# A mixture-of-experts tail: the first expert's rows before most slabs, the last small expert joined on chip

## The chip, the cores and the metric

One core of one Trainium2 chip runs the whole kernel in one launch. The metric is the device time of that launch in microseconds, lower is better. TensorE, VectorE, ScalarE, GpSimd and SyncE each run their own stream of instructions and meet at semaphores; GpSimd and SyncE mostly issue DMAs.

## The reference

Two layers of a hybrid decoder on 512 prompt tokens and 8 sample tokens of width 1024. The mixers (windowed attention, gated linear attention) and the dense feed-forward of layer 0 are as before and untouched. The second layer ends in a mixture of 8 experts of which each token uses 2:

```python
def _moe(h, rw, rb, wg, wu, wd):
    logits = (h @ rw + rb).astype(jnp.float32)
    top_v, top_i = lax.top_k(logits, TOP_K)
    probs = jax.nn.softmax(top_v, axis=-1)
    gates = jnp.sum(jax.nn.one_hot(top_i, N_EXPERTS, dtype=jnp.float32) * probs[..., None], axis=1).astype(h.dtype)
    out = jnp.zeros_like(h)
    for e in range(N_EXPERTS):
        out = out + gates[:, e:e + 1] * _swiglu(h, wg[e], wu[e], wd[e])
    return out
...
    x = x + g2 * f.reshape(b, s, d)
```

## The kernel before

`x` stays in SBUF, features on partitions: [128, 8, 520], 512 prompt columns and 8 sample columns. All matrix products with weights are done three times with operands split into a high and a low part: each slab of weights (128 x 1024, 512 KB) is loaded, ScalarE copies its high part, VectorE subtracts to get the low part, TensorE multiplies.

The experts (`experts(l)` in each engine's block) work on rows, not on all tokens. The experts are ranked by how many tokens chose them; the four larger ones get 256 rows, the four smaller ones 128. A DRAM tensor `slots` holds 384 rows for each pair of a large and a small expert. A program value `n_sweeps` says how often all experts are gone through, once for these inputs. The steps:

1. TensorE turns the normalised tokens to rows, VectorE writes them to `hT` (five blocks, L1730), GpSimd writes these to `h_rows` in DRAM (L594) and gathers the first expert's 256 rows from there into `xs` (two indirect DMAs, L598). Then it scatters all rows, twice each, to `slots` (ten indirect DMAs, L606).
2. SyncE loads an expert's 33 slabs into a ring of 11 buffers (`raw` for three, `more` for eight, L491). A slab goes into its buffer when the slab 11 before it has been split (`slab_low`). `first_slabs` loads the first three slabs of an expert as soon as its number is known; it stands before the loop and once more at the end of each sweep, where it loads three slabs that nobody multiplies.
3. TensorE turns `xs` (`to_features`, L762), ScalarE and VectorE split it into `XE`. In `expert(i, half)` TensorE does 22 slabs of gate and up products (L802), turns the hidden rows (L782), and 11 slabs of down products (L820) into the PSUM banks 4 to 7. In between (`next_features`) it turns the rows of the expert that comes next, also in the last one. The splits run ahead of TensorE by at most six slabs, and by at least three (`AHEAD`).
4. The result `Yo_large` or `Yo_small` is evacuated (L1374, L1849), GpSimd writes it back to `slots` (L619), after which it fetches the `xs` of the next large expert (L617).
5. After the last small expert GpSimd gathers for each block of 128 tokens (`TAIL`: the samples first) the two rows of each token from `slots` into `Yg` (L625). ScalarE scales one by its gate (L1384), VectorE adds the other (L1858), TensorE turns the sum (L836), VectorE multiplies by the modulation and adds to `x` (L1873), GpSimd writes the block to the output `yT` (L631).

Each engine goes through its own list in the order of the code, and a wait holds back all that stands behind it on that engine.

Of the kernel before, what the change touches and what calls it, by code (L numbers as in the profile page):

```python
# [14 lines left out]
F32 = mybir.dt.float32  # L15
# [87 lines left out]
def build(nc, xT, cT, wst, cst, sml, wa2, kcT, vc, st, yT, kp, vp, sp_, ks, vs, ss):  # L103
    ctx = ExitStack()
    with ctx:
# [25 lines left out]
        def fixed(name, shape, dt=F32):  # L131
# [66 lines left out]
        sweeps = at("sweeps", [P, 1], I32, H0 + 31680)  # L198
# [26 lines left out]
        Yg = [[at(f"Yg{n}{q}", [P, D], F32, (B0 + 8192 * n if n < NB else Z0) + 4096 * q)  # L225
               for q in range(CHOICES)] for n in range(NB + 1)]
        ysm = at("ysm", [P, KT, NS], F32, Z0 + 8192)
# [150 lines left out]
        TAIL = (NB,) + tuple(range(NB))  # L378
# [79 lines left out]
        def _(sp):  # L458
# [42 lines left out]
            n_sweeps = sp.value_load(sweeps[0:1, 0:1], min_val=1, max_val=3)  # L501
            with sp.Fori(0, n_sweeps) as c:
# [5 lines left out]
                first_slabs(c + 1)  # L508


        @block.gpsimd
        def _(pool):
# [97 lines left out]
            n_sweeps = pool.value_load(sweeps[0:1, 0:1], min_val=1, max_val=3)  # L610
            with pool.Fori(0, n_sweeps * RANKS) as i:
                for half in range(2):
                    pool.wait_ge(sem("xt_done"), i * 6 + (4 + 2 * half))
                    if half == 0:
                        pool.dma_start(xs[:, 0:1, :], slot_rows(i * PAIR_ROWS + CAPS[0], 1)).then_inc(sem("xs_in"), 16)
                    else:
                        pool.dma_start(xs[:], slot_rows(i * PAIR_ROWS + PAIR_ROWS, 2)).then_inc(sem("xs_in"), 16)  # L617
                    pool.wait_ge(sem("Yo_made"), i * 3 + (3 + half))
                    pool.dma_start(slot_rows(i * PAIR_ROWS if half == 0 else (i + 1) * PAIR_ROWS - CAPS[1], 2 - half), Yo[half][:]).then_inc(sem("Yo_out"), 16)  # L619
                    pool.wait_ge(sem("Yo_out"), i * 32 + (16 + 16 * half))  # L620

            for n in TAIL:
                rows = block_rows(n)
                for q in range(CHOICES):
# [3 lines left out]
            for n in range(NB):  # L628
                pool.wait_ge(sem("x_final"), n + 2)
                cols = slice(n * P, n * P + P if n + 1 < NB else N)  # L630
                pool.dma_start(yT[:, :, cols], x[:, :, cols]).then_inc(sem("y_out"), 16)  # L631
# [9 lines left out]
        def _(pe):  # L641
# [95 lines left out]
            def experts(l):  # L737
# [31 lines left out]
                def expert(i, half):  # L769
# [23 lines left out]
                    for c in range(CHUNKS):  # L793
                        cols = chunk_cols(c)
                        pe.wait_ge(sem("hel_made"), i * (2 * CHUNKS) + (c0 + c + 1))
                        for k in range(4 * c, chunk_end(c) + 1):
# [12 lines left out]
                            if half == 1 and k in (10, 12, 14, 16):  # L809
                                next_features((k - 10) // 2)  # L810
# [1582 lines left out]
```

## Time and profile before

| | us |
|---|---|
| median of 3 timed runs | 1932.15 (1929.97 to 1937.15) |
| profiled execution | 1930.32 |
| its span | 1928.8 |
| TensorE busy in it | 1823.4 (95%) |
| VectorE, ScalarE, GpSimd busy | 996.9, 810.8, 115.5 |
| mean granted TensorE clock | 0.969 |

The span is from the first to the last instruction; the execution is 1.5 us longer. The share of TensorE is a mean over a long product part and two short parts around the experts in which it waits. A granted clock of 1.00 is 2.4 GHz, 0.50 is 1.2 GHz. Times of an instruction overlap with those of its neighbour where an engine is pipelined, so the distance of starts is what a series costs.

### The profile page before, as it was taken

Reading aid. Unit: us, or ns where it says so; the run is one execution under the profiler, and the core shown is the slowest. Engines: PE = TensorE matmul, PEld = TensorE weight load, DVE = VectorE, ACT = ScalarE, POOL = GpSimd, SP = SyncE. Lnnn points to the kernel's source line nnn. Section 1 sums busy time; section 2 is a strip of 40 time slices with the busy share of each in tenths; the row PEclk is TensorE's granted clock in tenths of the full one; section 3 lists DMA queues with packets and bytes.
Section 4 is the critical chain, followed back from the end, with each engine's and each line's share of the span. In section 5 each row is a group of like instructions: output and inputs, shape, how many; then the busy total and the mean of one; then the engine's idle time right before and its main releaser. Section 6 shows DMA issues by size and latency. Waiting matters only on the chain.

```text
span 1928.8 us, 33321 instructions
## 1 busy us (share of the span) xinstructions
PE 1823.4 (95%) x13468; PEld 1638.8 (85%) x13468; DVE 996.9 (52%) x1380; ACT 810.8 (42%) x1192; POOL 115.5 (6%) x170
## 2 busy tenths in 40 slices
PE   6999999999999999999999999959999999999993
PEld 4888999998998999989889999948878878878872
DVE  4367552745222323335675527455495495495483
ACT  3346524323221122224465243225375385385471
POOL 1000010001101100000000100020000000000002
PEclk8999999999999999999999999969999999999996
DMA  9832235247676742224222342166596596596574
GB/s 376 346 113 91 97 135 199 89 153 252 223 254 205 252 164 88 86 80 154 69 88 100 135 177 100 45 270 235 174 371 239 174 360 244 179 348 250 185 283 143
DMA packets 96905, 362.94 MB, mean 188 GB/s; under 512 B 12212, under 2 KB 12244, under 8 KB 94992
## 3 DMA queue, kind: packets, MB, share of 16 engines
q1 hardware_dynamic: 65376, 238.94, 34.7%
q0 software_dynamic: 31408, 122.27, 17.6%
q8 instruction: 90, 1.47, 0.3%
q14 instruction: 31, 0.25, 0.0%
HBM read 310.80 MB, written 50.36 MB: 187 GB/s over the span
## 4 chain that ended last, share of the span: by engine, by line
PE 81%; DMA 7%; DVE 4%; issue 3%; ACT 3%; SPq 1%; POOL 0%; POOLq 0%; ACTq 0%; DVEq 0%
PE ps L650 46%; PE ps L802 16%; PE ps L820 9%; DMA xs<-slots 2%; PE ps L842 2%; DMA g<-gates 2%; DMA slots<-Yo_large 1%; DMA first_ada<-weights 1%; PE ps L762 1%; SPq L464 1%; PE ps L782 1%; PE ps L1080 1%; ACT scb L1491 1%; PE ps L958 1%; PE ps L970 0%
## 5 line engine op out<-in xcount | busy, mean ns | idle before, releaser
L650 PE MATMUL ps<-Hh,wh 128*128 128x260 f32 x2080 | 604.4, 291 | 9.4 <-ACT qrt L1520 5.3
L650 PE MATMUL ps<-Hl,wh 128*128 128x260 f32 x2080 | 592.9, 285 | 0.0
L650 PE MATMUL ps<-Hh,wl 128*128 128x260 f32 x2080 | 592.0, 285 | 0.0
L650 PEld LDWEIGHTS ps<-Hh,wh 128*128 128x128 f32 x2080 | 397.1, 191 | 29.5 <-issue 28.6
L650 PEld LDWEIGHTS ps<-Hh,wl 128*128 128x128 f32 x2080 | 397.3, 191 | 0.0
L650 PEld LDWEIGHTS ps<-Hl,wh 128*128 128x128 f32 x2080 | 396.9, 191 | 0.2
L1673 DVE TENSOR_TENSOR wl<-raw,wh 128x1024 fp32r<-128x1024 f32 x168 | 205.5, 1223 | 337.8 <-ACT wh L1305 337.4
L1305 ACT ACTIVATE wh<-raw 128x1024 fp32r<-128x1024 f32 x168 | 177.2, 1055 | 215.6 <-PE ps L650 212.6
L802 PE MATMUL ps<-further,XE 128*128 128x512 f32 (+1 forms) x840 | 189.2, 378 | 0.0
L802 PE MATMUL ps<-wh,XE 128*128 128x512 f32 (+1 forms) x592 | 181.8, 379 | 1.9 <-issue 1.9
L802 PEld LDWEIGHTS ps<-further,XE 128*128 128x128 f32 x840 | 146.6, 188 | 29.1
L1807 DVE TENSOR_TENSOR wl<-more,wh 128x1024 fp32r<-128x1024 f32 x96 | 115.8, 1223 | 42.4 <-ACT wh L1332 42.1
L1807 DVE TENSOR_TENSOR further<-more,further 128x1024 fp32r<-128x1024 f32 x96 | 115.9, 1224 | 36.6 <-ACT further L1332 36.5
L802 PEld LDWEIGHTS ps<-wh,XE 128*128 128x128 f32 x592 | 109.4, 190 | 21.6 <-issue 2.3
L1332 ACT ACTIVATE wh<-more 128x1024 fp32r<-128x1024 f32 x96 | 99.8, 1056 | 41.5 <-PE ps L802 22.3
L802 PE MATMUL ps<-wl,XE 128*128 128x512 f32 (+1 forms) x296 | 110.9, 375 | 0.0
L650 PE MATMUL ps<-hidh,wh 128*128 128x260 f32 x352 | 101.3, 288 | 4.8 <-issue 3.2
L1332 ACT ACTIVATE further<-more 128x1024 fp32r<-128x1024 f32 x96 | 99.7, 1055 | 14.1 <-PE ps L820 8.4
L650 PE MATMUL ps<-hidl,wh 128*128 128x260 f32 x352 | 99.4, 282 | 0.0
L650 PE MATMUL ps<-hidh,wl 128*128 128x260 f32 x352 | 99.3, 282 | 0.0
L820 PE MATMUL ps<-further,heh 128*128 128x512 f32 x256 | 81.2, 398 | 0.0
L650 PEld LDWEIGHTS ps<-hidh,wh 128*128 128x128 f32 x352 | 66.3, 188 | 10.4 <-DVE hidl L2256 5.5
(407 smaller groups left out, 2627.4 us busy)
## 6 DMA issues: line engine op xcount, KB each, us to landing
raw<-weights SPq DMA_DIRECT2D x243, 512.0 KB, 3.5
more<-weights SPq DMA_DIRECT2D x192, 512.0 KB, 5.2
ada<-weights POOLq DMA_DIRECT2D x16, 1536.0 KB, 8.1
slots<-nothing POOLq DMA_DIRECT2D x28, 704.0 KB, 12.8
first_ada<-weights POOLq DMA_DIRECT2D x8, 2048.0 KB, 12.5
gates<-stage POOLq DMA_DIRECT2D x32, 260.0 KB, 2.8
first_ada<-weights SPq DMA_DIRECT2D x16, 512.0 KB, 16.0
g<-gates POOLq DMA_DIRECT2D x2, 3120.0 KB, 12.4
```

Of the source, the lines that this page charges most:

```text
L464: sp.dma_start(first_slab(m), wst[m, :, :]).then_inc(ada_full[m], 16)
L650: mm = pe.matmul(out, w, v[:, cols], start=first and q == 0, stop=last and q == 2)
L762: mm = pe.transpose(ps[:, 4 + r, k * P:k * P + P], xs[:, r // 2, (4 * (r % 2) + k) * P:(4 * (r % 2) + k) * P + P], ident)
L782: mm = pe.transpose(ps[:, 2 * (c % 2), (b * tiles + t) * P:(b * tiles + t) * P + P], hmm[:, c % 2, t, b * P:b * P + P], ident)
L802: mm = pe.matmul(ps[:, 2 * (c % 2) + t, 0:cols], X[:, v, kk, t * P:t * P + P], w[:, b * cols:b * cols + cols], start=kk == 0 and r == 0, s ...
L820: mm = pe.matmul(ps[:, 4 + 2 * t + q, :], v[:, k, t * P:t * P + P], w[:, q * 512:q * 512 + 512], start=k == 0 and r == 0, stop=k == FE - 1 ...
L842: mm = pe.matmul(ps[STRIP * j:STRIP * j + STRIP, bank, 0:SCOLS], c_pad[:, m % CHUNK, :], w[:, j * SCOLS:j * SCOLS + SCOLS], start=m % CHUN ...
L958: mm = pe.transpose(ps[:, 6, h * P:h * P + P], scb[t % 4][:, h, c * P:c * P + P], ident)
L1305: act.activation(wh[:, sl, :], raw[:, sl, :], ACT.Copy).then_inc(hi_made[sl], 1)
L1332: act.activation(split_pair(k % SPLITS)[0], ring(k % EXP_SLABS % RING), ACT.Copy).then_inc(sem("slab_high"), 1)
L1673: dve.tensor_tensor(wl[:, sl, :], raw[:, sl, :], wh[:, sl, :].bitcast(F32), ALU.subtract).then_inc(split_made[sl], 1)
L1807: dve.tensor_tensor(w_l, ring(k % EXP_SLABS % RING), w_h.bitcast(F32), ALU.subtract).then_inc(sem("slab_low"), 1)
```

## The change

On SyncE one wait is added between the first three slabs and the rest, and the output is written by SyncE in four parts. On the other engines the last pair of experts is written out apart from the loop (`final=True`):

- During the last large expert VectorE works out, from row numbers and gates, for each token whether one of its two rows lies in the last small expert's 128 rows (`last_rows`): `w_others` are the gates with those rows set to 0, `last_of` is a token by row matrix holding the gate at the row's place. TensorE turns it and ScalarE copies it to `last_to` (128 rows x 520 tokens).
- The gathers from `slots` follow the write of `Yo_large`, before the last small expert's rows have been multiplied. The samples' gather waits until TensorE has finished the gate and up products, since it lands in `XE[1]`.
- The last small expert turns no next rows, and the last three splits are left out. ScalarE and VectorE scale and mix `Yg` with `w_others` after their last split.
- After the last product TensorE turns `Yg` into banks of 512 tokens each, and multiplies `Yo_small`, straight from SBUF, by `last_to`; VectorE adds both to `x`, 512 columns at a time.

```diff
             first_slabs(0)
             sp.wait_ge(sem("order_made"), 1)
             n_sweeps = sp.value_load(sweeps[0:1, 0:1], min_val=1, max_val=3)
+            sp.wait_ge(sem("xs_in"), 32)
             with sp.Fori(0, n_sweeps) as c:
...
                 first_slabs(c + 1)
+            sp.wait_ge(*dve_tail("samples_final"))
+            for k in range(0, KT, 2):
+                sp.wait_ge(*dve_tail(f"x_final{k + 1}"))
+                sp.dma_start(yT[:, k:k + 2, :], x[:, k:k + 2, :]).then_inc(sem("y_out"), 16)
+            sp.wait_ge(sem("y_out"), 16 * (KT // 2))
...
+            with pool.Fori(last, last + 1) as i:
+                small_rows(i, True)
+            for n in range(NB + 1):
                 rows = block_rows(n)
+                if n == 0:
+                    pool.wait_ge(*pe_tail("last_turned"))
+                if n == NB:
+                    pool.wait_ge(*pe_tail("gates_done"))
...
                     pe.wait_ge(sem("XE_made"), i * 6 + (4 + 2 * half))
+                    if final and half == 0:
+                        pe.matmul(ps[:, 6, 0:P], ones, MSK, start=True, stop=True).then_inc(sem("pe_tail"), 1)
...
-                            if half == 1 and k in (10, 12, 14, 16):
+                            if half == 1 and k in (10, 12, 14, 16) and not final:
                                 next_features((k - 10) // 2)
-
-                    pe.wait_ge(sem("XE_made"), i * 6 + (6 + 4 * half))
+                            if final and half == 0 and k == 8:
+                                pe.wait_ge(*dve_tail("last_of_made"))
+                                for n in range(NB):
+                                    pe.transpose(ps[:, 7, n * P:n * P + P], last_of[:, n, :], ident)
+                                pe.transpose(ps[:, 6, 0:NS], last_of[0:NS, NB, :], ident[0:NS, 0:NS]).then_inc(sem("pe_tail"), 1)
...
+                for n in range(NB):
+                    pe.wait_ge(sem("f_made"), n + 1)
+                    for k in range(5):
+                        main_turned(n, k)
+                pe.wait_ge(sem("f_made"), NB + 1)
+                for k in range(KT):
+                    mm = pe.transpose(ps[:, 7, k * NS:k * NS + NS], Yg[NB][0][0:NS, k * P:k * P + P], ident[0:NS, 0:NS])
+                mm.then_inc(sem("pe_tail"), 1)
+                pe.wait_ge(sem("Yo_made"), last * 3 + 4)
...
+                for k in range(5, KT):
+                    if k > 5:
+                        pe.wait_ge(*dve_tail(f"x_main{k - 6}"))
+                    for n in range(NB):
+                        main_turned(n, k)
+                for k in range(KT):
+                    if k in (0, 4):
+                        pe.wait_ge(*dve_tail("samples_final" if k else "samples_main"))
+                    else:
+                        pe.wait_ge(*dve_tail(f"x_main{k + 1 if k < 4 else k}"))
+                    pe.matmul(ps[:, LAST_BANK[k], :], Yo[1][:, 0, k * P:k * P + P], last_to[:, 0:T], start=True, stop=True
+                              ).then_inc(sem("pe_tail"), 1)
...
                     for k in range(EXP_SLABS):
-                        slab_high(i, s0 + k + AHEAD)
+                        if not (final and half and k + AHEAD >= EXP_SLABS):
+                            slab_high(i, s0 + k + AHEAD)
...
-                dve.tensor_scalar(sweeps[:], posv[8][:, 0, 0:1], 1.0, None, ALU.add).then_inc(sem("order_made"), 1)
+                link(dve.tensor_scalar(sweeps[:, 1:2], posv[8][:, 0, 0:1], float(RANKS), float(RANKS - 1), ALU.mult, ALU.add))
+                dve.tensor_scalar(sweeps[:, 0:1], posv[8][:, 0, 0:1], 1.0, None, ALU.add).then_inc(sem("order_made"), 1)
...
+                    for n in range(NB + 1):
+                        rows = block_rows(n)
+                        link(dve.tensor_scalar(last_of[0:rows, n, :], ps[0:rows, 6, 0:P], at_last[0:rows, n:n + 1], None, ALU.is_equal))
+                        mm = dve.tensor_scalar(last_of[0:rows, n, :], last_of[0:rows, n, :], w_last[0:rows, n:n + 1], None, ALU.mult)
+                    mm.then_inc(sem("dve_tail"), 1)
...
+                        if final and half == 0 and k == 2:
+                            last_rows()
...
+                def added(bank, k):
+                    return dve.scalar_tensor_tensor(out=x[:, k, 0:T], in0=ps[:, bank, :], scalar=mod[:, l, 5 * KT + k, 0:1],
+                                                    in1=x[:, k, 0:T], op0=ALU.mult, op1=ALU.add)
```

SyncE at the entry, before the change (`ISA` rows hold a wait or set up a DMA; the line numbers are those of each kernel):

```order
L491 DMA raw<-weights 128x1024
L501 TENSOR_LOAD sweeps [waits order_made]
L501 ISA x2
L502 UNCONDITIONAL_BRANCH
L504 TENSOR_LOAD eids
L504 ISA x2
L506 ISA
L491 ISA [waits slab_low]
```

and with it:

```order
L513 DMA raw<-weights 128x1024
L523 TENSOR_LOAD sweeps [waits order_made]
L523 ISA x2
L525 UNCONDITIONAL_BRANCH [waits xs_in]
L527 TENSOR_LOAD eids
L527 ISA x2
L529 ISA
L513 ISA [waits slab_low]
L513 DMA more<-weights 128x1024
```

The first slab for `more` now stands behind a wait for `xs_in`, the gathered rows.

GpSimd at the exit, before the change:

```order
L619 ISA [waits Yo_made]
L619 DMA slots<-Yo_small 128x1024
L620 REGISTER_ALU
L611 ISA [waits Yo_out]
L611 COMPARE_AND_BRANCH
L625 DMA Yg_180<-slots,rowi 8x1024
L625 DMA Yg_181<-slots,rowi 8x1024
L625 DMA Yg_172<-slots,rowi 128x1024
...
L631 DMA yT<-x 1024x1x128 [waits x_final] x3
L631 DMA yT<-x 1024x1x136 [waits x_final]
```

and with it:

```order
L642 DMA xs<-slots 128x1024
L644 REGISTER_ALU
L645 ISA [waits xt_done]
L646 ISA [waits Yo_made]
L646 DMA slots<-Yo_large 128x2x1024
L647 ISA
L656 ISA [waits Yo_out]
L656 COMPARE_AND_BRANCH
L665 DMA Yg_172<-slots,rowi 128x1024 [waits pe_tail]
L665 DMA Yg_173<-slots,rowi 128x1024
...
L665 DMA Yg_180<-slots,rowi 8x1024 [waits pe_tail]
```

The gathers follow the write of `Yo_large`, not of `Yo_small`; the fetch of two tiles of `xs` and the writes of `yT` are gone from GpSimd.

TensorE after the last product, before the change (L836 turns `Yg`):

```order
L820 MATMUL ps<-further_166,hel 128x512
L836 MATMUL ps<-cs,Yg_180 128x8 [waits f_made]
L836 MATMUL ps<-cs,Yg_180 128x8 x7
L836 MATMUL ps<-cs,Yg_172 128x128 [waits f_made]
L836 MATMUL ps<-cs,Yg_172 128x128 x7
...
L836 MATMUL ps<-cs,Yg_176 128x128 [waits x_final,f_made]
L836 MATMUL ps<-cs,Yg_176 128x128 x7
...
L105 UNCONDITIONAL_BRANCH
```

and with it:

```order
L864 MATMUL ps<-further_166,hel 128x512
L880 MATMUL ps<-cs,Yg_172 128x128 [waits f_made]
L880 MATMUL ps<-cs,Yg_172 128x128 x4
...
L890 MATMUL ps<-cs,Yg_180 128x8 [waits f_made]
L890 MATMUL ps<-cs,Yg_180 128x8 x7
L892 REGISTER_ALU
L894 MATMUL ps<-last_to,Yo_small 128x8 [waits Yo_made]
L894 MATMUL ps<-last_to,Yo_small 128x8 x7
...
L880 MATMUL ps<-cs,Yg_172 128x128 [waits dve_tail]
...
L906 MATMUL ps<-last_to,Yo_small 128x512 [waits dve_tail] x8
L105 UNCONDITIONAL_BRANCH
```

The turning of the tokens' rows moves ahead of everything that needs the last small expert, whose rows come in as products with `last_to`; for features 5 to 7 and for these products TensorE waits for banks that VectorE has read.

## Rows read from the trace of the kernel before

**Rows 1.** Windows: stretch: us, busy of each engine, clock, DMA share, GB/s.

```profile
1700.00:1800.00 100.00, 98.61 (x474) 81.34 (x473) 69.94 (x75) 62.60 (x75) 1.11 (x2) 1.00 0.79 289
1900.00:1929.00 29.00, 7.87 (x32) 6.27 (x32) 13.67 (x38) 4.60 (x4) 7.24 (x8) 0.50 0.53 184
```

**Rows 2.** Timeline, GpSimd at the entry: start, us, what, idle before and releaser.

```profile
1275.48 0.53 POOL L594 DMA_DIRECT2D h_rows<-hT  x1 [0.64 <-DVE hT L1730]
1284.87 1.02 POOL L598 DMA_INDIRECT xs<-h_rows,first_rows  x1 [8.86 <-DMA h_rows<-hT]
1286.20 0.98 POOL L598 DMA_INDIRECT xs<-h_rows,first_rows  x1 [0.30 <-issue]
```

**Rows 3.** Timeline, SyncE's DMAs at the entry.

```profile
1269.28 1.39 SPq L491 DMA_DIRECT2D raw<-weights  x3
1272.23 5.66 SPq L491 DMA_DIRECT2D more<-weights  x8
1282.85 2.60 SPq L491 DMA_DIRECT2D raw<-weights  x3
```

**Rows 4.** Timeline of TensorE at the entry, then the chain that ended last.

```profile
1294.89 3.68 PE L762 MATMUL ps<-cs,xs 128*128 128x128 f32 x16 [17.52 <-DMA xs<-h_rows,first_rows]
...
1300.49 18.38 PE ps L802 x72
```

**Rows 5.** Windows, DMA engines at the entry.

```profile
1280.00:1283.00 3.00, 0.00 (x0) 0.00 (x0) 2.17 (x9) 2.71 (x3) 0.00 (x0) 0.50 1.02 418
```

**Rows 6.** Chain that ended last, last small expert: start, us, what.

```profile
1842.73 10.28 DMA xs<-slots
...
1853.13 0.65 PE ps L762 x4
...
1856.57 0.44 PE ps L762 x4
...
1873.99 12.50 PE ps L820 x54
```

**Rows 7.** SyncE's DMAs in the last small expert, and windows there.

```profile
1851.91 13.36 SPq L491 DMA_DIRECT2D more<-weights  x8
1866.68 2.93 SPq L491 DMA_DIRECT2D raw<-weights  x3
...
1866.00:1869.00 3.00, 3.00 (x19) 2.63 (x18) 3.00 (x4) 2.60 (x4) 0.00 (x0) 1.00 1.02 408
...
1872.00:1875.00 3.00, 3.00 (x16) 2.40 (x15) 2.83 (x5) 2.53 (x4) 0.00 (x0) 1.00 0.28 115
```

**Rows 8.** Instructions on the tile more, from 1830: ScalarE's, first and last start.

```profile
L1332 ACT ACTIVATE further<-more x12: 1046/1056/1067, 1838.8 to 1878.2; 128x1024 fp32r<-128x1024 f32 x12
```

**Rows 9.** Timeline of the exit.

```profile
1886.51 1.02 ACT L1374 ACTIVATE Yo_small<-ps 128x1024 f32<-128x1024 f32 x1 [3.14 <-PE ps L820]
...
1903.75 0.22 DVE L1869 TENSOR_TENSOR ysm<-ps,mod 128x64 f32<-128x64 f32 x1
...
1909.49 1.15 ACT L1384 ACTIVATE Yg<-Yg,r 128x1024 f32<-128x1024 f32 x1 [1.36 <-DMA Yg<-slots,rowi]
...
1918.14 0.85 POOL L631 DMA_DIRECT2D yT<-x  x1 [1.20 <-DVE x L1873]
```

**Rows 10.** Chain that ended last, exit: one write and one gather.

```profile
1888.25 2.93 DMA slots<-Yo_small
...
1895.93 5.10 DMA Yg<-slots,rowi
```

**Rows 11.** Timeline of VectorE in layer 0: eight additions of 520 columns.

```profile
29.08 5.46 DVE L1896 SCALAR_TENSOR_TENSOR tn<-x,mod,ri 128x520 f32<-128x520 f32 x8
```

**Rows 12.** Timeline of TensorE in layer 1: f32 products, both operands unsplit.

```profile
927.66 1.04 PE L701 MATMUL ps<-qsq,cs 128*128 128x260 f32 x4
```

**Rows 13.** DMA issues: KB each, median us to landing.

```profile
raw<-weights SPq DMA_DIRECT2D x243, 512.0 KB, 3.5
...
yT<-x POOLq DMA_DIRECT2D x3, 512.0 KB, 3.8
```

More of the change, by code:

```diff
@@ new lines, in experts, with main_turned @@
+                for half in range(2):
+                    expert(last, half, True)
+                def main_turned(n, k):
+                    mm = pe.transpose(ps[:, MAIN_BANK[k], n * P:n * P + P], Yg[n][0][:, k * P:k * P + P], ident)
+                    if n == NB - 1:
+                        mm.then_inc(sem("pe_tail"), 1)
+                for n in range(NB):
+                    pe.wait_ge(sem("f_made"), n + 1)
+                    for k in range(5):
+                        main_turned(n, k)
@@ L1375, in expert @@
                                    ).then_inc(sem("Yo_made"), 1)
-                with act.Fori(0, n_sweeps) as c, act.Fori(0, RANKS) as e2:
+                last = act.value_load(sweeps[0:1, 1:2], min_val=RANKS - 1, max_val=3 * RANKS - 1)
+                with act.Fori(0, last) as i:
                     for half in range(2):
-                        expert(c * RANKS + e2, half)
-                for j, n in enumerate(TAIL):
-                    rows = block_rows(n)
-                    act.wait_ge(gathered[n], 32)
-                    act.activation(Yg[n][0][0:rows, :], Yg[n][0][0:rows, :], ACT.Copy, scale=r1[7][0:rows, n, :]
-                                   ).then_inc(sem("f_half"), 1)
+                        expert(i, half)
+                for half in range(2):
+                    expert(last, half, True)
             act.wait_ge(sem("c_landed"), 16)
@@ L1833, in expert @@
                     for k in range(EXP_SLABS):
-                        slab_low(i, s0 + k + AHEAD)
+                        if not (final and half and k + AHEAD >= EXP_SLABS):
+                            slab_low(i, s0 + k + AHEAD)
+                        if final and half == 0 and k == 2:
+                            last_rows()
                         if k % 4 == 1 and 5 <= k <= 21:
@@ L1856, in mix @@
+                for half in range(2):
+                    expert(last, half, True)
+                for n in range(NB + 1):
                     rows = block_rows(n)
-                    dve.wait_ge(sem("f_half"), j + 1)
-                    dve.scalar_tensor_tensor(out=Yg[n][0][0:rows, :], in0=Yg[n][1][0:rows, :], scalar=r1[8][0:rows, n, :],
+                    dve.wait_ge(sem("f_half"), n + 1)
+                    dve.scalar_tensor_tensor(out=Yg[n][0][0:rows, :], in0=Yg[n][1][0:rows, :], scalar=w_others[0:rows, 1, n:n + 1],
```

166 lines of the change are left out of this document (106 added, 60 removed).

## Prediction, made before the change was run

> **What bounds the kernel now.** I read the stretches first [rows 1]: inside the experts TensorE is busy 98.61 of 100 us at the full clock, while the last 29 us have it busy for 7.87 us at half clock. So a change inside the experts pays only what it takes out of TensorE's own stream, and one at either edge pays in full. The two edges are the entry to the first expert (GpSimd, SyncE and TensorE around 1260 to 1305 us [rows 2 to 4]) and the way out of the last one [rows 9, 10]. In between, only the last small expert differs from its three forerunners, and there the DMA engines are the second resource at their limit [rows 7].
>
> Entry: TensorE waits 17.52 us for the first expert's rows and starts its first product at 1300.49 [rows 4]. The wait has two parts. GpSimd issues the last write to h_rows at 1275.48 but its gathers only at 1284.87, because the writes land late, and the second gather (1286.20) lands 8.7 us later [rows 2, 4]. Beside them SyncE has put eight slabs of 512 KB on the DMA engines at 1272.23 and three more at 1282.85 [rows 3], and the engines are full, at 418 GB/s [rows 5].
>
> Exit: the last product ends at 1886.49 [rows 6], ScalarE takes Yo_small out [rows 9], then come its write to slots, ten gathers, scaling, mixing, turning and adding block by block, and the write of yT. From 1886.5 to the span's end are 42.3 us.
>
> **The change, part by part.**
>
> *Entry.* Eight slabs leave the queue until the gathered rows are in. The three early slabs were issued by 1270.7 and are gone when the last writes are made. An undisturbed write of 512 KB takes 2.93 us [rows 10]; two overlap, so I take 3.5 us, and h_rows is complete at 1275.48 + 3.5 = 1279.0 instead of about 1284.7: 5.7 us. For a gather with only gathers behind it the row says 5.10 us [rows 10] against 8.7 now: 3.5 us less, but the gathers start with only their successors beside them, and between 5.1 and 6 us are possible; I take 2.7. Sum 8.4. VectorE has one more small chained step ahead of order_made, 0.2 us. Net **-8.2 us**. Ends: 5.5 us if the gather still takes its 8.7 us and the step is paid, 9.5 us if writes take 2.93 us and the gather 5.1.
> What is queued behind SyncE's new wait is slabs 3 to 10, and ScalarE's splitting waits for them. TensorE would begin at 1292.3; now its first six slabs take 18.38 us, 3.1 each [rows 4], so slab 3 must be split by 1301.5 and landed some 2.5 us before. The rows are in at about 1286.7; slab 3 is issued then. GpSimd's ten scatters run beside it. Even if the slabs had only the 100 GB/s that a software transfer gets beside slabs in rows 6 (1 MB in 10.28 us), 512 KB would take 5.2 us, and with the 2.93 us of an undisturbed transfer on top it lands at 1295. I cost this at nothing; the cover is the three slabs already split, and without them it would be the 8 us from 1286.7 to 1295.
>
> *Last large expert.* TensorE gets one 128x128 product and five transposes. Four transposes cost 0.44 us of its chain [rows 6], so some 0.11 each: **+0.7 us**. VectorE gets about 12 small chained steps and ten of 128 columns, 5 to 6 us, ScalarE two evacuations. Both lead TensorE by up to six slabs of some 3 us here, so they hide; with no lead the price would be 5 us.
>
> *Last small expert.* There are no next rows to turn. Now TensorE idles for them (the row's 0.65 includes the fill, 1.2 us of idle before it) and turns four groups at 0.65, 0.44, 0.44 and 0.44 us [rows 6]: 3.2 us. I take **-3.1 us**. VectorE loses four steps too, so it should keep up; it works nearly without pause here, hence a low end of 1 us.
> The two halves of the last iteration also lose three splits of slabs nobody multiplies, which frees ScalarE before the end. Its last useful split starts at 1878.2 [rows 8], 8.3 us before the last product ends.
>
> *The gathers beside the last small expert.* Eight gathers, 4.2 MB, start when Yo_large has landed, in the trace at 1842.7 where the 1 MB fetch of xs starts now [rows 6]. SyncE issues slabs until 1865.3 and three at 1866.68 that nobody multiplies [rows 7]. The engines are full until about 1872.5 (408 GB/s, then 115) [rows 7]. The change adds 4.2 MB and takes 1 MB away: 3.15 MB at 0.41 MB per us are 7.7 us, full until about 1880. If software transfers keep the 102 GB/s of rows 6, slabs get 300, one per 1.75 us, where TensorE takes one per 1.39 (54 products, nine slabs, in 12.50 us [rows 6]). From the times in rows 7 a slab is issued eleven splits ahead of its use, about 15 us, and that stock falls by 0.15 slab per us: about 3 slabs by 1865, no stall. The last gather lands at about 1880, on the same scale on which the last product ends at 1883.4 once 3.1 us are gone. ScalarE's scaling (1.15 us [rows 9]) and VectorE's mixing of the last blocks then end at about 1884.4, under the transposes of the earlier ones. Cost taken: 0, with up to 7.7 us if all of the added traffic came before the work it delays.
> The Trainium skill (DMA: Bandwidth & Descriptors, SWDGE vs HWDGE vs iDMA) says that each DMA engine takes turns between its software and its hardware queues. Equal turns would bring the gathers in by 1863 and leave the slabs 209 GB/s, one per 2.5 us, a stock of some 3 slabs at the worst; rows 6 and 7 show one quarter for the software side, not half, and the measurement decides. By that rule late gathers would be impossible and a late slab a little likelier; the sum is the same.
>
> *Exit.* From the end of the last product (0): TensorE turns 20 blocks already mixed, 0.11 each, 2.2; eight small ones, under 0.8; so VectorE starts at 3.1. Its chain is then samples (two steps of 0.22 us, 0.5 with the hand-over) [rows 9], five additions, samples again 0.5, three and eight additions of 512 columns. Eight steps of this kind and 520 columns took 5.46 us, 0.68 each [rows 11], so 16 x 0.68 = 10.9. End at 3.1 + 1.0 + 10.9 = 15.0. The last eight products (f32, 512 columns) must keep ahead. Four f32 products of 260 columns took 1.04 us with the first one's fill, so about 0.22 each [rows 12], and 0.43 for 512 columns; they wait for VectorE, not the reverse. At half clock (0.85 us) TensorE would end at 16.7, and VectorE with the transposes doubled too at 18: the far end, +3 us. Yo_small's evacuation, 1.0 us [rows 9], runs beside the transposes. SyncE then writes the last quarter: 3.5 us as for a slab [rows 13], against 3.8 for yT now. Last, yT landed at 1918.14 + 3.85 = 1922.0 and the span ended at 1928.8: 6.8 us that stay. Sum 15.0 + 3.5 + 6.8 = 25.3 instead of 42.3: **-17.0 us**. Ends 14 and 18.5.
>
> Total: -8.2 + 0.7 - 3.1 - 17.0 = **-27.6 us**. The profiled execution took 1930.32 us (span 1928.8), so it would be 1902.7; the median of the three timed runs is 1932.15, so I forecast 1904.5.
>
> **Rivals.**
> *A, the join is late* (0.13). The last gathers or a late slab hold TensorE or ScalarE in the last small expert. For it: full DMA engines, VectorE without pause. Against: the issue of slabs ends 21 us before the last product. Price 4 to 10 us: 1908 to 1915.
> *B, the entry does not gain* (0.06): the writes to h_rows are slow for a reason other than the slabs. Then only the gather is faster, -2.5 instead of -8.2: 1910.
> *C, the last small expert falls to half clock* (0.03). If slabs come at 2.5 us each, TensorE pauses after each; the rows of the exit now show 0.50 once it pauses [rows 1]. Its 33 slabs of 1.39 us are 45.9 us at the full clock; at a mean granted clock c they grow by 45.9/c - 45.9. From c = 0.62 down that eats the whole 27.6 us, and at 0.50 the time is 1904.5 + 45.9 = 1950, slower than before. Against: the stock of slabs above; TensorE kept 98.61 of 100 us beside the same kind of traffic.
> *D, mixed small losses* (0.04): VectorE's chain in the last large expert not hidden (+5), added to B (+5.7) and the dear end of A (+10): a gain of 7 us, about 1925.
>
> **How the numbers follow.** The forecast has 0.74: 1904.5, alone from 1898.5 (entry 9.5, small expert 3.2, exit 18.5, that is -30.5, with 3 us for the spread of the timed runs, whose lowest is 2.2 below their median) to 1912 (entry 5.5, exit 14, small expert 1). With A and B taken in and D and C left out the range is 1897 to 1914. A measurement of this kernel can tell 0.5% (9.7 us) from no change, so faster means below 1922.5: forecast, A and B, 0.93. Same: D, 0.04. Slower: C, 0.03.
>
> **What would show it.** After: TensorE's first expert product near 1292; h_rows complete near 1279; slabs 3 to 10 issued from 1286.6 with no wait of ScalarE for one. TensorE without the 1.2 us pause in the last small expert, gathers landed before ScalarE's last split, clock 1.00 there. From the last product to the end about 25 us, VectorE in sixteen additions of about 0.68 us. It is wrong if ScalarE waits for gathered rows beyond the last product, if TensorE waits for slab_low anywhere in the last pair, or if the first gather still takes over 8 us.

## The result, and the profile after

The changed kernel takes 1900.91 us (median; 1900.40 to 1901.69), the kernel before, measured with it, 1932.51 us: a ratio of 0.9839, 95% interval 0.9819 to 0.9859. That is 31.6 us less; the forecast was 1904.5, 27.6 us less. The profiled execution took 1900.92 us, its span is 1899.3 us.

The two profiled executions don't reach the entry at the same time. The last write to h_rows is issued at 1275.48 before [rows 2] and at 1277.72 after, 2.2 us later, for work that the change does not touch; among the profiled executions of this document that issue falls anywhere from 1274.6 to 1280.8. So I measure from there: before 653.3 us to the end of the span, after 621.6, a difference of 31.7, as the medians have it.

Four pieces make it up, each from rows below:

| piece | before | after | difference | forecast |
|---|---|---|---|---|
| last h_rows issue to first expert product | 25.01 | 17.26 | -7.75 | -8.2 |
| first product to end of last product | 586.0 | 586.98 | +1.0 | -2.4 |
| end of last product to end of span | 42.3 | 17.34 | -25.0 | -17.0 |
| sum | 653.3 | 621.6 | -31.7 | -27.6 |

**Entry.** Timeline of GpSimd and SyncE there (start, us, what, in brackets the idle time and what ended it), kernel after:

```profile
1271.35 1.39 SPq L513 DMA_DIRECT2D raw<-weights  x3
...
1277.72 0.53 POOL L622 DMA_DIRECT2D h_rows<-hT  x1 [0.63 <-DVE hT L1806]
1282.87 1.02 POOL L626 DMA_INDIRECT xs<-h_rows,first_rows  x1 [4.62 <-DMA h_rows<-hT]
1284.20 1.74 POOL L626 DMA_INDIRECT xs<-h_rows,first_rows  x1 [0.30 <-issue]
...
1290.88 5.50 SPq L513 DMA_DIRECT2D more<-weights  x8
```

The chain that ended last (start, us, what), kernel after:

```profile
1284.20 5.41 DMA xs<-h_rows,first_rows
...
1294.98 8.08 PE ps L838 x26
```

GpSimd waits 4.62 us for its writes, where it waited 8.86 [rows 2], and the second gather takes 5.41 us, where it took 8.7 (from 1286.20 [rows 2] to TensorE's start at 1294.89 [rows 4]). These are the lines that answer to the two halves of the entry's term. (The whole chain of this execution puts the first gather down to VectorE's row numbers, made at 1282.57, which the scatters need. The last write lands at 1282.60. In nine of the profiled executions, before and after among them, the first gather starts 0.27 us behind the last landing, whenever the row numbers were made; so the landing holds it.)

The slabs that now start at 1290.88 are late for ScalarE, though not for TensorE. Timeline of ScalarE, kernel after:

```profile
1296.56 1.28 ACT L1401 ACT_TABLE_LOAD   x1 [2.54 <-DMA more<-weights]
...
1301.35 1.06 ACT L1401 ACTIVATE further<-more 128x1024 fp32r<-128x1024 f32 x1 [1.49 <-DMA more<-weights]
...
1307.37 1.06 ACT L1401 ACTIVATE wh<-more 128x1024 fp32r<-128x1024 f32 x1 [2.43 <-DMA more<-weights]
```

TensorE is busy 100.00 of the 100 us from 1300 to 1400 in this execution: the three slabs split beforehand and the lead of the splits covered it. They don't always. Six of the nine other profiled executions below that have the wait show TensorE waiting 0.54 to 2.23 us once, some 19 to 21 us behind its first product. One of them, timeline of TensorE and chain in the kernel with held gathers and early mixing:

```profile
1316.72 0.68 PE L817 MATMUL ps<-cs,hmm 128*128 128x128 f32 x4 [1.92 <-DVE hmm L1933]
```

```profile
1298.88 13.98 DMA more<-weights
...
1312.97 0.05 ACT wh L1402
...
1315.34 0.61 ACT sgm L1417
```

ScalarE stands at a slab that lands at 1312.9, and the activation `sgm`, which TensorE needs next, stands behind it in ScalarE's list.

**Last small expert.** Timeline, TensorE's waits and one of ScalarE's, kernel after:

```profile
1839.96 0.44 PE L816 MATMUL ps<-cs,hmm 128*128 128x128 f32 x2 [1.03 <-DVE hmm L1921]
...
1863.95 0.44 PE L816 MATMUL ps<-cs,hmm 128*128 128x128 f32 x2 [0.64 <-DVE hmm L1921]
...
1866.57 1.06 ACT L1401 ACTIVATE further<-more 128x1024 fp32r<-128x1024 f32 x1 [1.79 <-DMA more<-weights]
...
1869.14 0.33 PE L816 MATMUL ps<-cs,hmm 128*128 128x128 f32 x1 [1.98 <-DVE hmm L1921]
```

And the chain that ended last:

```profile
1849.03 17.44 DMA more<-weights
...
1869.47 12.49 PE ps L864 x54
```

Read these two against [rows 6]: the long DMA of this chain was the fetch of xs, and is now a slab, 17.44 us from issue to landing. VectorE's hmm is named as the releaser of TensorE, but VectorE itself stood behind ScalarE's split of that slab. Of the ring's slabs eight land between 1843.7 and 1863.7, one per 2.5 us; in the same stretch GpSimd's gathers are on the DMA engines. What each side moved (packets, MB, share of the engines' time; hardware are SyncE's slabs, software are GpSimd's transfers), kernel after from 1845 to 1863:

```profile
q1 hardware_dynamic: 1024, 3.74, 52.0%
q0 software_dynamic: 1000, 3.64, 50.4%
```

**Exit.** The chain gives the end of the last product, 1869.47 + 12.49 = 1881.96. Timeline of VectorE, TensorE and SyncE behind it, kernel after:

```profile
1884.77 0.22 DVE L1970 TENSOR_TENSOR ysm<-ps,mod 128x64 f32<-128x64 f32 x1 [1.27 <-PE ps L890]
...
1885.17 3.38 DVE L1966 SCALAR_TENSOR_TENSOR x<-ps,mod,x 128x512 f32<-128x512 f32 x5
...
1887.82 7.03 PE L906 MATMUL ps<-last_to,Yo_small 128*128 128x512 f32 x16
...
1888.85 7.33 DVE L1966 SCALAR_TENSOR_TENSOR x<-ps,mod,x 128x512 f32<-128x512 f32 x11
...
1892.31 4.24 SPq L535 DMA_DIRECT2D yT<-x  x4
```

VectorE starts 2.8 us behind the last product and works without a pause to 1896.18, 14.2 us behind it. The last quarter of yT is issued at 1896.2 and lands 2.7 us later; the span ends 0.4 us after that. Before, 6.8 us lay there. TensorE's granted clock from 1884 to 1888 is 1.00.

### The profile page after: what moved, and what is told of

Its sections match the earlier page's. It is cut to its first block, busy times and chain, and to the rows that moved or that the text cites. A ratio compares the mean times of both kernels' runs of the same rounds, so it can differ in the third digit from the quotient of the medians.

```text
span 1899.3 us, 33332 instructions
## 1 busy us (share of the span) xinstructions
PE 1829.6 (96%) x13491; PEld 1641.8 (86%) x13491; DVE 997.6 (53%) x1383; ACT 802.8 (42%) x1185; POOL 119.8 (6%) x164
## 3 DMA queue, kind: packets, MB, share of 16 engines
q0 software_dynamic: 30416, 118.57, 17.3%
## 4 chain that ended last, share of the span: by engine, by line
PE 82%; DMA 7%; DVE 4%; issue 3%; ACT 3%; SPq 1%; POOL 0%; DVEq 0%; POOLq 0%; ACTq 0%
PE ps L685 47%; PE ps L838 15%; PE ps L864 9%; PE ps L911 2%; DMA g<-gates 2%; DMA xs<-slots 2%; DMA more<-weights 1%; DMA first_ada<-weights 1%; DMA slots<-Yo_large 1%; SPq L486 1%; PE ps L796 1%; PE ps L816 1%; PE ps L1149 1%; ACT scb L1567 1%; PE ps L1027 1%
```

## The experiments

My theory after the result had four parts: the entry gains because slabs no longer share the DMA engines with writes and gathers; the exit gained 6.8 - 0.4 us more than forecast because GpSimd no longer issues the last DMA; the last small expert gained nothing because the gathers take half of the DMA engines from the slabs; and the rest of the exit is VectorE's sixteen additions. Times below are medians; the kernel before measured 1931.95 to 1933.33 in the three groups of runs. The kernel after was measured in a group of its own, so a difference of 1 or 2 us from it says little, and spans counted from the last h_rows issue are given where they matter. Edits are against the kernel after unless it says before.

### Who issues the last DMA

```diff
-            sp.wait_ge(*dve_tail("samples_final"))
-            for k in range(0, KT, 2):
-                sp.wait_ge(*dve_tail(f"x_final{k + 1}"))
-                sp.dma_start(yT[:, k:k + 2, :], x[:, k:k + 2, :]).then_inc(sem("y_out"), 16)
-            sp.wait_ge(sem("y_out"), 16 * (KT // 2))
+            for j in range(AHEAD):
+                sp.wait_ge(more_full[j], 416)
...
+            pool.wait_ge(*dve_tail("samples_final"))
+            for k in range(0, KT, 2):
+                pool.wait_ge(*dve_tail(f"x_final{k + 1}"))
+                pool.dma_start(yT[:, k:k + 2, :], x[:, k:k + 2, :]).then_inc(sem("y_out"), 16)
+            pool.wait_ge(sem("y_out"), 16 * (KT // 2))
```

SyncE's list then ends with a wait for its three last slab loads, which is over long before.

> The kernel after, with one thing undone: the four yT writes at the end are issued by GpSimd and not by SyncE; their shape and what they wait for stay. In the trace of after, 0.4 us lie between the landing of the last write and the end of the span; before, 6.8 us did. Theory A: those 6.8 us belong to a program whose last DMA is issued by GpSimd. Then this kernel is 6 to 7 us slower than after, about 1907, the time lying behind the landing. Theory B (rival): they belonged to the larger write that came last before (four token blocks and samples, 512-byte pieces in another order) or to the run. Then it stays within 1 us of after, 1900 to 1902.

Measured 1909.28 us (1908.22 to 1910.76), 8.4 us above after. The mirror image, before with its four writes moved from GpSimd to SyncE:

> The kernel before, with one thing done: the block writes of yT are issued by SyncE and not by GpSimd, shapes and waits unchanged. Theory A (the end costs 6.8 us where GpSimd issues the last DMA): 6 to 7 us faster than before, about 1926, and under 1 us between the last landing and the end. Theory B (the shape of the write or the run): within 1 us of before, 1931 to 1933.

Measured 1925.99 us, 7.3 us below before (ratio 0.9959, 0.9948 to 0.9971). The rows that decide are the last issues (first and last start) and the landing times; first after with GpSimd, then before with SyncE:

```profile
L673 POOL DMA_DIRECT2D yT<-x x4: 534/553/598, 1893.3 to 1896.9; - x4
...
DMA to landing us min/median/max: 3.0/3.6/3.8
```

```profile
L512 SPq DMA_DIRECT2D yT<-x x4: 533/537/662, 1909.7 to 1918.4; - x4
...
DMA to landing us min/median/max: 3.6/3.6/3.7
```

After with GpSimd: the last write, issued at 1896.9, lands 3.7 us later at 1900.6, and the span is 1907.8: 7.1 us behind the landing. Before with SyncE: 1918.4 + 3.7 = 1922.1, span 1922.5: 0.4 us. The shape of the write follows the kernel and the tail follows the issuing engine, so the rival is out. The engine that issues the last write is in all four kernels also the one that waits for its landing; which of the two roles brings the tail was not tried. Of the 8.4 us, about 6.7 are the tail and 1.0 the slower landing.

### The wait at the entry

Taken out of after (one line, SyncE's `sp.wait_ge(sem("xs_in"), 32)` ahead of the ring's slabs), and put alone into before:

> The kernel after, with SyncE's wait for the first expert's gathered rows taken out: the ring's slabs are again issued as soon as their buffers are free, while the two gathers keep their new place ahead of the last three slabs. Theory A (the wait is what the entry's gain comes from; the kernel before with the wait alone became 7 to 9 us faster): 6 to 8 us slower than after, about 1908, with the second gather landing some 8 us after its issue. Rival (the new order of GpSimd and ScalarE at the entry carries the gain too): less than 3 us slower.

> The kernel before, with one line of the change: SyncE issues the slabs of the ring only after the first expert's gathered rows have landed. It does the entry part alone, less the reordering that lets the two gathers stand ahead of three slabs. Theory A: the entry's gain is that the gather of xs does not share the DMA engines with queued slabs; the first expert product comes 6 to 8 us earlier, the kernel is 6 to 8 us faster (about 1925), and no later wait gives it back. Rival: the slabs that now start later are missing in the first large expert; TensorE waits there, and half of the gain or more is given back (1928 to 1933).

Without it 1911.98 us, 11.1 above after; before with it 1924.72, 8.6 below before (ratio 0.9964, 0.9942 to 0.9986, so 2.7 to 11.2 us). Timelines of GpSimd and TensorE, after without the wait, then before with it:

```profile
1286.35 1.28 POOL L625 DMA_INDIRECT xs<-h_rows,first_rows  x1 [8.73 <-DMA h_rows<-hT]
...
1296.69 3.65 PE L795 MATMUL ps<-cs,xs 128*128 128x128 f32 x16 [17.54 <-DMA xs<-h_rows,first_rows]
...
1302.77 0.79 PE L837 MATMUL ps<-wh,XE 128*128 128x512 f32 x1 [2.43 <-issue]
```

```profile
1280.41 1.02 POOL L599 DMA_INDIRECT xs<-h_rows,first_rows  x1 [5.25 <-DMA h_rows<-hT]
...
1287.03 3.68 PE L763 MATMUL ps<-cs,xs 128*128 128x128 f32 x16 [10.41 <-DMA xs<-h_rows,first_rows]
```

The old waits, 8.73 and 17.54 us, are back to a tenth of a microsecond with the wait gone; counted from the last h_rows issue, this profiled execution is 10.3 us longer than that of after. 8.4 of them are lost by the first product (25.68 us behind that issue in place of 17.26), 0.8 in the first large expert, and 1.1 in the exit, where the granted clock is 0.50 from 1896 to 1899, for a reason that no run here shows. The expectation of 6 to 8 us was too low by that. The new order of the gathers and the last three slabs shows no gain on its own. In before with the wait, TensorE waited once for a late slab, 0.54 us at 1311.42: the first product came 17.7 us behind the last h_rows issue, and the profiled span, counted from that issue, is 5.8 us shorter: 7.3 gained at the entry, 1.5 given back behind it, of which 1.0 in the first large expert.

### Gathers against slabs

One line on GpSimd, ahead of the gathers beside the last small expert:

```diff
+                pool.wait_ge(sem("slab_used"), i * PAIR_SLABS + (SPLITS + EXP_SLABS + 10))
```

> The kernel after, where GpSimd holds the gathers of the output rows until TensorE has used ten of the last small expert's twenty-odd slabs. Nothing else changes. In the trace of after ScalarE waits five times for slabs in that expert while GpSimd's gathers run, and TensorE waits 0.64 and 1.98 us behind it, where the forecast had 3.1 us gained. Theory A: the gathers take half of the DMA engines' time from the slabs; with them held, the slabs land in time, the two waits of TensorE go, 2 to 3 us faster than after (1898 to 1899), unless the gathers then land too late for the turns at the end. Rival: the waits come from ScalarE's and VectorE's own work there; then it stays within 0.7 us of after, and TensorE's two waits stay.

Measured 1901.13 us (1899.49 to 1908.75): the time of after, which by the total would have been a miss for theory A. The chain that ended last says otherwise:

```profile
1856.66 16.73 DMA more<-weights
...
1873.49 1.07 ACT further L1402
...
1875.81 5.98 DVE Yg L1963 x5
...
1881.83 0.66 PE ps L891 x8
```

And windows of the same kernel (busy of TensorE, its weight loads, VectorE, ScalarE, GpSimd, then clock, DMA share, GB/s):

```profile
1860.00:1865.00 5.00, 5.00 (x34) 4.58 (x33) 4.74 (x7) 4.48 (x7) 1.48 (x2) 1.00 1.02 406
1865.00:1870.00 5.00, 5.00 (x23) 4.01 (x23) 4.00 (x5) 2.46 (x4) 1.04 (x1) 1.00 1.03 410
...
1884.00:1888.00 4.00, 4.00 (x17) 3.58 (x18) 3.97 (x9) 0.00 (x0) 0.00 (x0) 0.50 0.00 0
```

TensorE is busy for 5.00 of 5 us where after shows it for 4.36 and 3.02, and the expert, from its first product to the end of its last, takes 48.5 us in place of 51.5: the forecast's 3.1 us, to a tenth. They were given back behind it. The last slab lands at 1873.4, ScalarE and VectorE mix gathered rows only after it, TensorE waits three times for mixed rows (0.32, 0.43, 0.42 us), and a stretch of the exit runs at a granted clock of 0.50. The exit takes 21.8 us in place of 17.4, so more than the gain is given back; counted from the last h_rows issue this execution is 3.1 us longer than that of after. The medians agree to 0.2 us all the same; the slowest of the four executions took 1908.75 us. Two runs asked which part of this counts.

> The kernel after, without the three slab loads that SyncE issues at the end of the pass for a further pass which a single pass does not have (left out: loads that nothing here uses; a second pass would need them). They are 1.5 MB in the stretch where the trace of after shows the DMA engines full, 3.8 us at 411 GB/s. Theory A: the last small expert's slabs are late there only because the engines are full; with 1.5 MB fewer the waits of ScalarE behind 1866 shrink, TensorE's wait of 1.98 us shrinks or goes, 0.5 to 2 us faster. Rival: those loads are queued behind the expert's own slabs, so they take only what is left over; within 0.5 us of after.

> Held gathers and no loads for a further pass, together. With held gathers alone the last small expert took 48.1 us in place of 51.3, as the forecast had it, but the last three slabs came late (ScalarE waited 0.95, 1.51 and 2.09 us), the mixing of the gathered rows began only behind them, TensorE waited 1.2 us for it and its clock then fell to half: the time was that of after. Theory A: without the 1.5 MB the last slabs land in time, the mixing ends before the last expert product, the exit keeps the full clock: 2 to 4 us faster than after (1897 to 1899). Rival: the last slabs wait for the gathers, not for those loads; then the exit still begins with waits of about 1 us, and the time stays within 1 us of after.

The edit takes out the call `first_slabs(c + 1)` at the end of SyncE's pass. 1903.00 us (1900.63 to 1904.41) and 1901.94 us (1899.88 to 1906.00): neither is faster, so theory A missed in both; the first median is 2.1 us above after, more than its rival allowed, and no row shows why (counted from the last h_rows issue it is 0.8). The three loads that serve nothing are queued behind the ones that do: in after they land from 1876.4 to 1878.9, behind the last useful slab at 1875.1. With both edits the mixing still began at 1878.31 behind the last split, for VectorE works in the order it is given.

### Mixing ahead of the last slabs

ScalarE's scaling and VectorE's mixing of the first three blocks move ahead of the last three splits, one block ahead of each; the wait of the gathers stays as above.

```diff
                     for k in range(EXP_SLABS):
+                        if final and half and 0 <= k + AHEAD - (EXP_SLABS - 3) < 3:
+                            others(k + AHEAD - (EXP_SLABS - 3))
                         if not (final and half and k + AHEAD >= EXP_SLABS):
                             slab_high(i, s0 + k + AHEAD)
...
-                        for n in range(NB + 1):
+                        for n in range(3, NB + 1):
```

(`others(n)` is the old loop's body; VectorE's part has the same form.)

> The kernel after with the gathers held (until TensorE has used ten slabs of the last small expert), and with the scaling and mixing of the first three blocks of gathered rows (five of 1.06 us on ScalarE, five of 1.23 us on VectorE) taken ahead of the last three slab splits, one block ahead of each. Held gathers alone made the last small expert 3.2 us shorter, and the exit 4.6 us longer: ScalarE and VectorE waited 0.95, 1.51 and 2.09 us for the last slabs and mixed only behind them, TensorE waited 1.2 us for mixed rows and then ran at a granted clock of 0.50. Theory A: the late mixing is the whole reason; with it in those idle gaps the exit is again about 17.4 us at full clock, the kernel 2.5 to 3.5 us faster than after, about 1898. Rival: the gathered rows are not there yet at that point (landing 11 us behind an issue at 1846 to 1857); the splits wait behind them, and the time is that of after or worse, 1900 to 1904.

> As the other run with held gathers and early mixing, and without the three slab loads that only a further pass would use (left out: they serve nothing in a single pass). Theory A (late mixing was the limit): 2.5 to 4 us faster than after; the 1.5 MB fewer bring at most 0.5 us beyond the other run, since the loads are queued behind the last slabs. Rival: the time of after.

> The kernel after with the early mixing alone; the gathers are issued at once, as in after. The slabs then still come late (half of the DMA engines' time goes to the gathers), TensorE waits 0.64 and 1.98 us in the last small expert, and the mixing was not late in after. Theory A: no change, within 0.7 us of after. Rival (the mixing is what keeps ScalarE and VectorE from the slabs): 1 to 3 us faster.

Measured 1898.05 us (ratio 0.9821, 0.9808 to 0.9835), 1898.21 us (0.9828, 0.9814 to 0.9841), and 1900.93 us for the early mixing alone (0.9837, 0.9823 to 0.9850). So 2.9 and 2.7 us by the medians for the pair of edits, as expected, and nothing for either alone. By the times alone this isn't certain: the intervals of the ratios overlap widely, and each of the two kernels has one execution above 1902 us, so that their means are only 2.0 and 2.5 us below that of the early mixing alone. The gain rests on the rows as well. Held gathers with early mixing, timeline of VectorE, then the chain:

```profile
1876.26 1.28 DVE L1901 SCALAR_TENSOR_TENSOR Yg<-Yg,w_others,Yg 128x1024 f32<-128x1024 f32 x1
1877.68 1.23 DVE L1890 TENSOR_TENSOR further<-more,further 128x1024 fp32r<-128x1024 f32 x1
```

```profile
1871.47 12.49 PE ps L865 x54
1883.96 2.18 PE ps L881 x20
```

The mixings stand between the splits, the expert takes 48.4 us, the exit from 1883.96 to 1901.3 takes 17.3 us, as in after, at a granted clock of 1.00. (This execution is the slowest of the five, 1902.93 us: it lost 3.7 us in the first large expert, in the 1.92 us pause shown at the entry and behind it, where the granted clock is 0.54 from 1317 to 1320.) In the kernel without the three loads the two stretches are 48.4 and 17.4 us as well, and the span, counted from the last h_rows issue, is 2.3 us shorter than after's, with a pause of 2.23 us in its first large expert. With the early mixing alone the expert is still 50.9 us long.

### One addition for each feature block

TensorE sums the turned rows and the last small expert's product in one PSUM bank, and VectorE adds eight times rather than sixteen; for that the turns become products with the identity. The samples are treated alike.

```diff
-                    mm = pe.transpose(ps[:, MAIN_BANK[k], n * P:n * P + P], Yg[n][0][:, k * P:k * P + P], ident)
+                    mm = pe.matmul(ps[:, MAIN_BANK[k], n * P:n * P + P], Yg[n][0][:, k * P:k * P + P], ident, start=n == 0, stop=False)
...
-                    pe.matmul(ps[:, LAST_BANK[k], :], Yo[1][:, 0, k * P:k * P + P], last_to[:, 0:T], start=True, stop=True
+                    pe.matmul(ps[:, MAIN_BANK[k], :], Yo[1][:, 0, k * P:k * P + P], last_to[:, 0:T], start=False, stop=True
```

> The kernel after, where the turned rows and the last small expert's product of one feature block are summed by TensorE in one PSUM bank, so VectorE adds once for each of the eight feature blocks and not twice; the turns become products with the identity. Theory A: VectorE's additions pace the exit of after (16 of 0.67 us from 1885.2 to 1896.2, of which about 8 would go); TensorE's part, 32 turns and 16 records of products, 2.35 + 0.66 + 1.95 + 1.51 + 7.03 = 13.5 us, becomes the pace, and the last addition ends about 14.2 us - 0.7 after the last expert product: the exit shortens by 0 to 2 us only. Rival: the products that ran 0.88 us each in after were held back by VectorE; at their own pace of 0.43 us per 512 columns the exit is 5 us shorter.

Measured 1906.43 us, 5.5 above after: both readings missed. Timeline of TensorE and VectorE:

```profile
1886.02 4.63 PE L879 MATMUL ps<-cs,Yg 128*128 128x128 f32 x40
...
1890.58 1.95 PE L889 MATMUL ps<-cs,Yg 8*128 8x8 f32 x16
...
1899.53 1.02 PE L901 MATMUL ps<-last_to,Yo_small 128*128 128x512 f32 x2
...
1900.59 0.75 DVE L1961 SCALAR_TENSOR_TENSOR x<-ps,mod,x 128x512 f32<-128x512 f32 x1 [1.00 <-PE ps L901]
```

Twenty turns are 20 records and 2.35 us as transposes, 40 records and 4.63 us as products: an f32 product counts twice. TensorE became the bound (VectorE waits 1.00 us before each of the last three), and the exit took 21.8 us. The expectation had carried the transposes' price over to the products. So in after both engines are near the pace: TensorE's sixteen records need 7.03 us beside eleven additions of VectorE in 7.33.

## Why the prediction was right, and where it was not

The time is inside the range and 3.6 us below the forecast; as differences, 31.6 against 27.6. The two edges gained, as forecast. The middle was to gain 2.4 us and lost 1.0, and the exit gained 8.0 more than forecast. That the total is so near is in part luck: the two errors have opposite signs.

*Entry, -8.2, measured -7.75.* The mechanism is the one given, shown from both sides by the runs with and without the wait. The two halves were sized wrongly and made it up: h_rows was to be complete 3.5 us after the last issue, and is only 4.9 us after it, since up to three writes still run at a time (their landing takes 4.9 us in the median after, 7.4 before); this gives 4.2 us and not 5.7. The gather was to give 2.7 and gave 3.2 (8.64 to 5.41). The scaling of rows into XE and its hand-over gave the last 0.4.

*No wait for slabs 3 to 10: wrong.* ScalarE waited five times, 9.4 us in all, for slabs that came one per 1.6 to 3.5 us. In the profiled execution of after the three split slabs and the time that ScalarE has over covered it, so its cost is the nought that was forecast, but I had named the cover and not counted the landing times behind the first slab. In six of the nine other profiled executions with this wait TensorE paused: 0.54, 0.81, 1.85, 1.92, 1.98 and 2.23 us. Five of their first large experts still took 96.8 to 97.6 us (96.6 to 96.8 where there was no pause; 96.2 before, and 96.6 in before with SyncE's writes), but in the sixth the granted clock fell behind the pause and it took 100.3. So the term is not nought on every execution, and the change can have a cost here that its own trace doesn't show.

*Last large expert, +0.7, measured +0.9* (95.4 us in place of 94.6). As given. The first large expert is 0.5 us longer, for which the forecast had no term; the five between give 0.2 back.

*Last small expert, -3.1, measured -0.2, and the gathers beside it, 0.* This is the step that failed. The 1.2 us pause went and the turns went, as said, but 0.64 and 1.98 us of new waits came. I had taken 102 GB/s for the gathers from the one fetch in [rows 6], and 300 for the slabs. In after eight slabs, 4.2 MB, landed in the 20.0 us to 1863.7: 210 GB/s, one per 2.5 us, against one per 1.39 that TensorE takes. That is the half share. The Trainium skill (DMA: Bandwidth & Descriptors, SWDGE vs HWDGE vs iDMA) says that each engine takes turns between its software and its hardware queues; here the trace agrees with it, with 3.74 and 3.64 MB from 1845 to 1863. The prediction had set it aside by a wrong reading of its own row: 10.28 us are the fetch's time from issue to landing, and not the time in which its packets moved. DMA queues of the kernel before, first from 1843 to 1846, then from 1847 to 1851:

```profile
q1 hardware_dynamic: 300, 1.10, 96.4%
...
xs<-slots POOLq DMA_DIRECT2D x1, 1024.0 KB, 10.3
```

```profile
q0 software_dynamic: 204, 0.84, 50.8%
q1 hardware_dynamic: 220, 0.80, 50.0%
```

The fetch is issued at 1842.73 and moves nothing before 1846; then it has half of the engines, about 200 GB/s, beside the slabs. So the trace of before showed the half share too. The eight gathers landed by 1866.3; equal turns had said 1863, the forecast 1880. What fills the 3 to 4 us behind the issue no run shows. The prediction's own working by equal turns still found a stock of three slabs and no stall, so the stock was taken too large as well. The runs show what it cost: with the gathers held the expert is 3.0 us shorter, 3.1 by forecast.

The list of what would show it said "wrong if TensorE waits for slab_low anywhere in the last pair". TensorE's waits stand against VectorE's hmm, and go back to it; it is the same fault under another name.

*Exit, -17.0, measured -25.0.* Sums from the end of the last product: VectorE begins at 2.8 (forecast 3.1), ends at 14.2 (15.0), the write takes 2.7 (3.5), and 0.4 follow (6.8). The first three terms hold within 0.8 us each. The last, "6.8 us that stay", is where the forecast lost 6.4: it was read as a fixed end of the program, and belongs to a program whose last DMA GpSimd issues and waits for. The pair of runs with the issuer exchanged shows it, +8.4 and -7.3. The change moved this write to SyncE, which the forecast had costed only by its landing. "0.43 us for 512 columns" of f32 was half of what it is, 0.88, because the four records of [rows 12] are two products; they kept ahead of VectorE, as it said, by less than a microsecond and not by half.

*The rivals.* A was there in kind, a late slab and no late gather, at 2.9 us and not 4 to 10. B is excluded. C did not occur in after; when the granted clock falls is open, see below. In the exit of after it is 1.00, as the sum took it.

## What to carry to other kernels

A tail behind the last landing is not a constant: look who issued the last DMA, and let SyncE do it where GpSimd would. Where the DMA engines are full, count GpSimd's transfers as half of their rate for as long as their packets move, read a rate from the windows and not from issue to landing, and hold the gathers until the stock of prefetched tiles can bear them; then look what else stood in program order behind the tiles that now come later, for the gain of one edit can be hidden until the second is made. A gain that doesn't show in the time may still be in the trace, one expert earlier. And a wait that costs nothing in one trace can cost 2 us in the next: look at every profile taken.

## What the runs showed of the hardware

- The end of the program: 6.8 and 7.1 us between the last landing and the end of the span where GpSimd issued the last DMA and waited for it, 0.4 us where SyncE did, in after and in before with SyncE.
- With both sides at work and the DMA engines full, SyncE's slabs and GpSimd's transfers moved 3.74 and 3.64 MB in 18 us in after, and 0.80 and 0.84 MB in 4 us in before.
- GpSimd's issue of one gather of 128 rows takes 0.94 us in the quiet, and 2.25 to 2.30 us in after from 1840 to 1850, where VectorE is busy 5.00 of each 5 us; with the gathers held it is 0.94 to 1.47 from 1846 to 1857, VectorE busy 4.95, 4.68 and 4.65 of each 5 us. A coincidence of rows, with little between 4.95 and 5.00; not tried by itself. Timeline of GpSimd, then a window, kernel after:

```profile
1840.76 2.25 POOL L665 DMA_INDIRECT Yg<-slots,rowi  x1 [0.30 <-issue]
...
1852.67 0.94 POOL L665 DMA_INDIRECT Yg<-slots,rowi  x1 [0.31 <-issue]
```

```profile
1845.00:1850.00 5.00, 5.00 (x25) 4.07 (x24) 5.00 (x7) 4.12 (x6) 4.39 (x3) 1.00 1.03 414
```

- An f32 product of TensorE runs as two records, a transpose as one: 0.88 us for 512 columns at a granted clock of 1.00, and 0.23 against 0.11 for 128.
- The granted clock fell to 0.50 for a stretch of the exit in four kernels: it was 0.50 from 1884 to 1888 with held gathers, from 1888 to 1890 with those and fewer loads, from 1886 to 1888 with the early mixing alone, and from 1896 to 1899 in after without the wait. It stayed at 1.00 in after, in both kernels with held gathers and early mixing, and in the other three that start from after. The first two had pauses of TensorE just before; the other two had none in the exit, the last ones were at 1868.04 and 1877.74, and their exits took 18.4 us in place of 17.4. After has such pauses in its last expert as well (the last at 1869.14) and kept the full clock. So the pauses don't explain it; what does stays open.
